# Issue order of key pages and value pages in one queue of a two-layer decoder kernel

## What is computed

```
past_k = cache_sb_k[j][page_table].reshape(db, n_pages * page, SB_HEADS, SB_HEAD_DIM)
past_v = cache_sb_v[j][page_table].reshape(db, n_pages * page, SB_HEADS, SB_HEAD_DIM)
z = einsum('bqhd,bkhd->bhqk', q, k) * scale + bias
log_fail = where(mask, log_sigmoid(-z), 0)
after = cumsum(log_fail, reverse=True) - log_fail
w = where(mask, exp(log_sigmoid(z) + after), 0)
out = einsum('bhqk,bkhd->bqhd', w, v)
```

## Time and profile before

| | us |
|---|---|
| median of 3 executions | 1794.27 |
| lowest, highest | 1792.76, 1803.53 |
| the profiled execution: its own time | 1795.47 |
| the profiled execution: span of its instructions | 1793.7 |
| TensorE busy | 1607.4 (90%) |
| VectorE busy | 753.8 (42%) |
| ScalarE busy | 630.6 (35%) |
| GpSimd busy | 568.7 (32%) |

### The profile page before, as it was taken

One profiled execution on the slowest core, in us unless ns is written; L12 is line 12 of the kernel. 1 busy time (PEld: TensorE's weight loads), 2 busy tenths in 40 slices (PEclk: granted clock), 3 DMA queues, 4 the chain that ended last, 5 costly groups with the idle time before them and its releaser, 6 DMA issues.

```text
span 1793.7 us, 25351 instructions
## 1 busy us (share of the span) xinstructions
PE 1607.4 (90%) x9409; PEld 1243.0 (69%) x9409; DVE 753.8 (42%) x1039; ACT 630.6 (35%) x1069; POOL 568.7 (32%) x472
## 2 busy tenths in 40 slices
PE   6679998786797998999989979999888999999997
PEld 4457665563475775767766546656568999999996
DVE  2561002324376767667767793014332321221221
ACT  3421223412224441444234342245533442342341
POOL 1221221100042433333333344322213444444443
PEclk9887899857798999999999989987799999999999
DMA  8472896843254889998996988621002233332322
GB/s 250 156 243 84 278 351 221 287 144 118 94 190 129 259 280 307 307 312 279 320 348 215 330 271 270 205 88 47 1 24 71 71 95 95 88 89 85 95 83 88
DMA packets 288755, 325.96 MB, mean 182 GB/s; under 512 B 13814, under 2 KB 205952, under 8 KB 288436
## 3 DMA queue, kind: packets, MB, share of 16 engines
q1 hardware_dynamic: 145800, 215.89, 36.3%
q10 hardware_dynamic: 140512, 100.67, 18.5%
q0 software_dynamic: 2320, 7.78, 1.2%
HBM read 315.48 MB, written 8.99 MB: 181 GB/s over the span
## 4 chain that ended last, share of the span: by engine, by line
PE 72%; DVE 11%; DMA 5%; ACT 5%; issue 3%; SPq 3%; POOL 1%; ACTq 0%; DVEq 0%; POOLq 0%
PE PS L513 46%; PE PS L527 5%; PE PS L552 3%; PE PS L472 2%; DMA wring<-w_ffn_up 2%; PE PS L822 2%; PE PS L462 2%; SPq L1210 2%; PE PS L1036 1%; DVE prod L2240 1%; DVE scr L1966 1%; DVE hl_r L1973 1%; PE PS L570 1%; PE PS L584 1%; DVE scr L2245 1%
## 5 line engine op out<-in xcount | busy, mean ns | idle before, releaser
L1334 POOL TENSOR_TENSOR parts<-wring,parts 128x512 fp32r<-128x512 f32 (+1 forms) x400 | 520.4, 1303 | 1106.6 <-ACT parts L1412 1106.0
L513 PE MATMUL PS<-hh_r,parts 128*128 128x260 f32 (+1 forms) x2880 | 716.7, 338 | 20.6 <-DVE hl_r L1973 11.6
L513 PEld LDWEIGHTS PS<-hh_r,parts 128*128 128x128 f32 x2880 | 494.7, 191 | 109.9 <-issue 53.4
L1412 ACT ACTIVATE parts<-wring 128x512 fp32r<-128x512 f32 (+1 forms) x400 | 248.0, 623 | 809.8 <-PE PS L513 681.0
L513 PE MATMUL PS<-hl_r,parts 128*128 128x260 f32 (+1 forms) x1440 | 462.5, 334 | 0.0
L513 PEld LDWEIGHTS PS<-hl_r,parts 128*128 128x128 f32 x1440 | 275.5, 191 | 27.6 <-issue 1.7
L513 PE MATMUL PS<-E_r,parts 128*128 128x260 f32 (+1 forms) x1584 | 261.8, 325 | 4.4 <-issue 2.4
L513 PEld LDWEIGHTS PS<-E_r,parts 128*128 128x128 f32 x1584 | 227.6, 191 | 43.6 <-issue 20.9
L2240 DVE TENSOR_TENSOR prod<-kring,PS 128x1024 f32<-128x1024 f32 x128 | 150.1, 1214 | 28.3 <-DMA kring<-cache_sb_k 28.0
L2245 DVE TENSOR_REDUCE scr<-prod 128x16 f32<-128x1024 f32 x128 | 149.7, 1211 | 0.0
L2422 DVE TENSOR_TENSOR xT<-xT,PS 128x512 f32<-128x512 f32 (+1 forms) x64 | 44.1, 690 | 199.1 <-PE PS L513 199.1
(11 more groups left out here) (313 smaller groups left out, 1560.3 us busy)
## 6 DMA issues: line engine op xcount, KB each, us to landing
vring<-cache_sb_v SPq DMA_DIRECT2D x256, 256.0 KB, 4.1
kring<-cache_sb_k SPq DMA_DIRECT2D x256, 256.0 KB, 4.2
wring<-w_ffn_up ACTq DMA_DIRECT2D x88, 512.0 KB, 5.3
wring<-w_ffn_down ACTq DMA_DIRECT2D x16, 1024.0 KB, 5.7
kring<-w_ffn_up SPq DMA_DIRECT2D x12, 1024.0 KB, 9.8
vring<-w_ffn_up SPq DMA_DIRECT2D x10, 1024.0 KB, 10.1
wring<-w_in_gla ACTq DMA_DIRECT2D x8, 1024.0 KB, 8.3
wring<-w_out ACTq DMA_DIRECT2D x8, 1024.0 KB, 5.0
```

What stands on the lines that cost most here:

```text
L513: last = mm(PS[:, bank + c, 0:w], parts[:, q, a, P * k:P * k + P], x[:, k0 + kk, o:o + w], start=(q == 0 and k == 0 and a == 0 and x is sr ...
L1334: gp.tensor_tensor(part_as(n, 1, src, w), src, part_as(n, 0, src, w), ALU.subtract).then_inc(wlo_ok, 1)
L1412: return fn(dst, src, ACT.Copy)
```

## The change

In SyncE's loop over the positions the two `while` loops change places. At each position at which a key group and a value group are both due, SyncE now waits for, and issues, the key group first. No instruction is added or taken away, and TensorE's, VectorE's, ScalarE's and GpSimd's streams are the same as before.

```diff
+                while kn < 64 and (sample_position(S_PANEL_STEP[68 + kn]) if kn < 2 else
+                                   kv_position(9 * ((kn - 2) // 8) + 1 + (kn - 2) % 8)) <= pos:
+                    k_pages(kn)
+                    kn += 1
                 while vn < 64 and (sample_position(S_PANEL_STEP[66 + vn]) if vn < 2 else
                                    kv_position(9 * ((vn - 2) // 8) + 13 + (vn - 2) % 8)) <= pos:
                     v_pages(vn)
                     vn += 1
-                while kn < 64 and (sample_position(S_PANEL_STEP[68 + kn]) if kn < 2 else
-                                   kv_position(9 * ((kn - 2) // 8) + 1 + (kn - 2) % 8)) <= pos:
-                    k_pages(kn)
-                    kn += 1
```

## The result

The changed kernel takes 1855.99 us (median of 4 executions, 1851.57 to 1859.43) against 1793.51 for the kernel before: a ratio of 1.0326, 95% interval 1.0296 to 1.0356, or 58 us (53 to 64) at 1794 us. It is not the quotient of these two medians, which lie 62.5 us apart; the expectations further down speak of the change's 62 us, the results of its 58. Forecast were 1838 us and slower, in a range of 1801 to 1869, which holds it; the size of the change was forecast as 43 us and is about 60.

A forecast was written before the change was run, and what follows sets the result against it. The prompt's matmuls on TensorE were taken as the pace, the page queue as a close second bound. New stalls 67, less 24 old waits, plus 9 clock, less 9 panels: 43 us on 1795.47, predicted 1838, range 1801 to 1869.

The forecast's parts named there:

- The mechanism: SyncE's queue: a value group behind a key group lands 12.0 us after VectorE's own step, so TensorE stalls.
- The lag: Up pieces: VectorE ends the step's key group 8.7 us after TensorE came to its value group.
- an absorbed lag: Rival: TensorE's stalls only close its distance to VectorE and don't add up; 1790 to 1810, some 1800; chance 0.12.
- the keys as the bound: Rival: keys come 3.44 us earlier, half of VectorE's 26.1 us wait may go; 13 us faster, 1782; chance 0.05.
- a queue that doesn't care: Rival: order within a position is lost in interleaving, or both slots are always free together; 1795; chance 0.05.
- the signs named: Among them: TensorE's value waits reach 50 us or more, ten to twenty places, 3 to 9 each; position 75, 6 to 9.
- The term for the up pieces: Positions 55, 59, 75, 79, 95, 99: value group late by 7.2 us at each, 6 x 7.2.
- the landing: Time from a group's last page issue until it has landed: taken as 5.5 us, range 4.1 to 7.3.
- The term for the down pieces: Three down stretches: value group late by 4.0 us at every third step, 2 places each, 6 x 4.0.
- What was taken off for old waits: Stretch 597 to 1093 us: TensorE's 9.6 us for values and 14.4 us of key transfers on the chain go; 24 off.
- The clock: TensorE runs slower after each of six longer stalls, 1.56 us each, 9 us more; four-microsecond stalls cost nothing.
- The weight panels: ScalarE's 36.5 us of waits for weight panels shrink by a quarter, 9 us off.

The follow-up runs named there:

- the up and the down part: Kernel before with the key group first only at up positions: 1.0167, 30 us slower; only at down positions: 1.0167, 30 us slower.
- the six and the rest: Kernel before with the key group first only at positions 53, 57, 73, 77, 93, 97: 1.0144; at every position except those: 1.0173.

## Why the prediction was right, and where its sizes were off

**The mechanism held.** SyncE's wait for the used key slot moved in front of the value group, and TensorE waits for the group where the prediction put it: at positions 55, 59, 75, 79, 95 and 99, and in the down stretches with two to four waits each (among them 87 and 90, a step of three apart). The lag was 8.7 us as worked out at five of the six up places (7.7 at the other), the issues 1.54, 3.44 and 1.55. The stalls add up: the up and the down part, and the six and the rest, each make the whole within their intervals. The rivals of an absorbed lag, of the keys as the bound, and of a queue that doesn't care are out.

The Trainium skill, "DMA: Bandwidth & Descriptors", section "Issuing engines are not separate DMA queues", has the time to initiate a DMA "usually small relative to the DMA itself". Here it is not: initiating a group takes 3.44 us and its transfer, by the estimate in the prediction, some 3.5.

Of the signs named, two did not come: the wait at position 75 is 4.95 us and not 6 to 9, and eight of the 18 waits are shorter than the 3 us named.

**The term for the up pieces was too high.** 6 x 7.2 us were put down, and the six waits make 29.1 us, 4.8 each. Two pieces of the term failed. One is the landing: 5.5 us from the last issue were taken, between the median and the ones on the chain, and it was 3.7 to 4.9, 4.2 in the mean, so 1.3 us less. The row of the median (4.1) would have given it. The other is the time until TensorE needs the group: 13.55 us were taken from one place, position 75, for all six, and it was 14.5 in the mean. At positions 59 and 79 it is 15.6, because TensorE has transposes (L831) there that wait for VectorE. The trace of the kernel before had it already; here are the value groups of its positions 77 and 79, 15.52 us apart, and what stands between:

```profile
783.16 1.06 PE L822 MATMUL PS<-vring,scr 128*32 128x512 f32 x8
...
792.03 1.13 PE L831 MATMUL PS<-ident,qcol 128*128 128x128 f32 x8 [1.03 <-DVE scr L2245]
...
798.68 1.06 PE L822 MATMUL PS<-vring,scr 128*32 128x512 f32 x8
```

**The term for the down pieces was too low in number.** 24 us in six places were put down. The changed kernel has ten outside the up pieces: 2.4, 1.8, 3.9 and 1.9 in the first stretch, 3.6 and 2.0 in the second, 4.1, 2.8 and 2.7 in the third, and 4.5 at position 121, past the stretches that I had looked at: 29.8 us. With the up pieces' 29.1 and two of under 1 us this is the 59.9 us of the waits. That the prediction's 67 us came near is luck in part, two errors of opposite sign.

**What was taken off for old waits was too much.** Of the 24 us, the 9.6 for values were rightly taken off, since the 59.9 us count every wait for values. The 14.4 us for key transfers on the chain were not a gain: VectorE does wait 13.5 us for keys where it waited 26.1, but the chain of the changed kernel still has 2.3% of 558 us in key transfers, 12.8 us, and TensorE's idle time other than for values fell by only 6.7 us, which the weight panels account for (below). This is the largest error of the sum. That less waiting by VectorE comes back as time was assumed, and no row showed it.

**The clock cost twice what was put down.** I gave 1.56 us to six stalls, 9 us, and nothing to those of about 4 us, for lack of a row and for no other reason. In the changed kernel TensorE is busy for 18.4 us more in the stretch with the same matmuls, at a granted clock of 0.93 instead of 0.98. Windows over the value group behind a wait of 4.95 us, and over one behind a wait of 3.6 us:

```profile
793.70:795.70 2.00, 1.97 (x9) 0.30 (x9) 2.00 (x3) 0.00 (x0) 0.00 (x0) 0.50 0.75 246
887.10:889.10 2.00, 1.94 (x9) 0.27 (x9) 1.85 (x2) 0.00 (x0) 0.00 (x0) 0.50 1.06 389
```

Both ran at 1.2 GHz. Eight of the 18 waits have a value group of 1.84 to 1.94 us behind them, after 3.6 to 5.9 us of standing. Behind four more, of 2.72, 2.76, 4.26 and 4.55 us, the clock fell within the value group or right behind it. That makes 12 waits, all those of 2.7 us and more, where the kernel before has two (of 4.86 and 2.37 us). The 18.4 us over ten more such waits are some 1.8 us each, an estimate near the 1.56 put down: the number of places was wrong more than the price. The clock term was not tested by a run of its own, so its share rests on the trace alone.

**The weight panels** were put down with 9 us off. TensorE's idle time other than for values fell by 6.7 us (43.6 us more idle, but 50.3 more of waiting for values). ScalarE's waits for the up panels fell from 25.8 to 9.9 us, those for the down panels (10.7) are gone, and TensorE's waits for the low parts made from the panels fell by 6.4 us. Before, 600 to 1093 us, and in the changed kernel, 600 to 1156 us:

```profile
PE PS L513 <- POOL parts L1334: 7.5, 4, 4.3
```

```profile
PE PS L513 <- POOL parts L1334: 1.1, 2, 0.7
```

The sum as it was measured in the stretch: 50.3 us more of waits for values, 6.7 less of other idle time, 18.4 of slower matmuls, 62 us. The prediction's 43 us had the new stalls 7.1 us too high. Against that it took off 14.4 us too much for old key waits and 2.3 too much for the panels, and put the clock 9.4 us too low. Together these make the 19 us that were missing.

## What to carry to other kernels

In a queue that waits in order, put first what its slot lets go first: before swapping two issues, compare for each when its slot comes free, and when its data is needed. Here the key slot came free 3 to 8 us after the value slot of the same step (783.5 against 775.8 at position 73), and the value group was needed two pieces later, so the order of two issues was worth 3%. What is left in front of a wait should be what needs no slot: reading the page numbers ahead of the wait gave 0.6% in the better order, and more than a third of the loss back in the worse one.

## What the runs showed that I had not expected

- A page transfer of 64 rows takes SyncE 469 ns to issue and one of 128 rows 333 ns, in all 512 page issues of each run by the median, so fetching less made the issue dearer.
- A value group at full speed behind a wait does not show that the clock stayed up. In the changed kernel the group behind a wait of 4.26 us took 1.09 us, but the matmuls right behind it ran at a granted clock of 0.50:

```profile
827.97 1.09 PE L822 MATMUL PS<-vring,scr 128*32 128x512 f32 x8 [4.26 <-DMA vring<-cache_sb_v]
```

```profile
829.05:832.15 3.10, 3.10 (x9) 2.43 (x9) 3.10 (x4) 0.00 (x0) 0.00 (x0) 0.50 0.35 128
```

- The length of the wait alone doesn't tell whether TensorE's clock falls. In the run with the wait and without the issue in front, a wait of 2.34 us was followed by a slow value group, and one of 2.57 us by one at full speed, with the clock at 1.00 for 9.5 us behind it:

```profile
877.81 1.72 PE L822 MATMUL PS<-vring,scr 128*32 128x512 f32 x8 [2.34 <-DMA vring<-cache_sb_v]
...
1049.46 1.06 PE L822 MATMUL PS<-vring,scr 128*32 128x512 f32 x8 [2.57 <-DMA vring<-cache_sb_v]
```

```profile
1050.50:1060.00 9.50, 9.50 (x42) 5.71 (x39) 8.03 (x8) 4.09 (x6) 2.57 (x2) 1.00 0.72 269
```

- With half the bytes of all pages left out, the kernel before gained only 5 us, though the DMA engines had been at 0.90 in this stretch and were at 0.73 then. So a busy share of 0.90 did not make their bytes the bound; the dearer issues hide some of what the bytes gave.

A third value slot would test the two-step distance directly. No run has it; it would take 8 KB more in each partition.
